# A hybrid attention and SwiGLU block on one core: three operand splits moved from VectorE to GpSimd, nine DMA copies and sums set later

## The chip, the cores and the metric

The kernel runs on 1 core of a Trainium2 chip. The metric is the device time of one execution in microseconds (us), lower is better. TensorE (PE) multiplies, VectorE (DVE), ScalarE (ACT) and GpSimd (POOL) work elementwise, and SyncE (SP) issues most DMAs. POOL also issues DMAs, those that add into DRAM among them. Every engine runs its own instructions in program order and waits on semaphores for the others.

## The reference, cut to what matters

One decoder block on 512 tokens of width 1024, float32. The part in question is the second half, after attention:

```python
h = rms_norm(x, norm2[l])
x = x + (jax.nn.silu(h @ w_gate[l]) * (h @ w_up[l])) @ w_down[l]     # D_FF = 2816
return rms_norm(x, final_norm)
```

## The kernel before

**Precision.** Each float32 operand of a matmul is split in two parts of the reduced type fp32r: a high part (a cast on ACT, `weights_hi`, L1188) and a low part, the difference of the operand and its high part. For weights the low part is taken by POOL (`split`, L765) or by DVE (`split_down` called from `split_own`, L1814). The list `by_dve` says for each chunk of weights which of the two does it. A product then takes three matmuls.

**Chunks.** The weights come in 148 chunks of 128x1024 numbers (512 KB), in one fixed order. SP loads each into one of three `raw` slots (more in the last stage). Chunk k is loaded once the low part of chunk k-3 is done, since this frees its slot. ACT casts it four chunks ahead of PE's use.

**The SwiGLU stage** has three parts. (1) Six tiles of 128 columns by plain products: chunks ("gate", f) and ("up", f), f = 0 to 5, 24 matmuls each. (2) Eight pairs of tiles in a Winograd form of Strassen's method with 7 products instead of 8: chunks ("mixed", (p, j)), p = 0 to 7 the pair and j = 0 to 6 the unit, 24 matmuls of 256 columns each. Below, m00 is ("mixed", (0, 0)), m05 is ("mixed", (0, 5)), m11 is ("mixed", (1, 1)) and so on. (3) The product with w_down, again in 7 products of 6 groups: chunks ("down", ...). The first down chunk is used after m76.

**Sums of weights.** Strassen's method needs sums of quarters of the weights. They are made in DRAM by DMA. `plan_sums` lists them as entries i = 0 to 55. An entry is a copy that SP issues (L715), right behind the load of chunk `copy_at[i]`, and then an accumulating DMA that POOL issues (`add_sum`, L786), in POOL's program behind chunk `add_at[i]`'s place. POOL waits there until the copy has landed. Entries 32 to 46 make the sums of w_down that use a copy: T3 (6 groups), T1 (6) and T2 (3). Nine more entries are added in place, later, and the change leaves them as they are.

**Order around the change.** In the loop over f on DVE, the low part of a chunk is taken four chunks ahead of PE: behind the tile f = 4 those of m00 and m01, behind f = 5 those of m02 and m03, in pair 0 at units 0, 1 and 2 those of m04, m05 and m06. `swiglu_tile(f)` (L1873 to L1883, L1820) multiplies gate and up and makes the forms for the last stage. `x_low` (L1863) takes the low parts of the activations' forms, which PE needs in pair 0: A11 and A12 behind f = 3, S2, S3 and A22 behind f = 4, S1 and S4 behind f = 5. Before `x_low` ACT makes the high parts (`x_high`, L1420), and ahead of these, at f = 4, `first_high` (L1406), which waits for L1874 on DVE. DVE's L1896 and L1905 take gate and up out of PSUM.

Of the kernel before, what the change touches and what calls it, by code (L numbers as in the profile page):

```python
# [54 lines left out]
SPLIT_SLOTS = 4  # L55
# [81 lines left out]
N_UNIT = len(UNITS)  # L137
BY_DVE = (0, 2, 4, 6)
# [39 lines left out]
def plan_chunks():  # L178

    chunks = []  # L180
    for kind, a in PROJ_JOBS:
        if kind == "h":
            chunks += [("w1", (a, q)) for q in range(4)]
        elif kind not in ("ht", "hc", "mt"):
            chunks.append((kind, a))
    chunks += [("o", (dh, kc)) for kc2 in (2, 0) for dh in range(2) for kc in (kc2, kc2 + 1)]
    fill = len(chunks)
    for f in range(F0):
        chunks += [("gate", f), ("up", f)]
    for p_ in range(N_PAIR):  # L190
        chunks += [("mixed", (p_, j)) for j in range(N_UNIT)]
    chunks += [("down", (n, g)) for n in range(N_PROD) for g in range(GROUPS_M)]
    return chunks, fill
# [29 lines left out]
def hymba_block(nc, x, norm1, w_in, lambda_q1, lambda_k1, lambda_q2, lambda_k2, diff_subln,  # L223
# [3 lines left out]
    chunks, n_fill = plan_chunks()  # L227
# [5 lines left out]
    todo = plan_sums()  # L233
    mixed0, down_from = n_fill + 2 * F0, n_fill + 2 * F0 + N_UNIT * N_PAIR
    copy_at = [6 + i for i in range(10)] + [27 + i // 2 for i in range(14)] + [KEYS_DONE] * 8
    copy_at += [n_fill + i for i in (0, 2, 4, 6, 7, 8, 9, 10, 11)] + [mixed0 + N_UNIT * i + 5 for i in range(6)]
    in_place = [down_from + GROUPS_M + i for i in range(COPIED_T2, GROUPS_M)] + [down_from + 3 * GROUPS_M + i for i in range(GROUPS_M)]
    add_at = copy_at[0:16] + [31] * 8 + [33] * 4 + [35] * 4 + copy_at[32:] + in_place
    assert len(add_at) == len(todo)
    by_dve = [c[0] == "down" or (c[0] == "mixed" and (c[1][1] in BY_DVE or c[1][0] == 0)) or (c[0] in ("gate", "up") and c[1] >= SPLIT_SLOTS // 2)  # L240
              for c in chunks]

    def late(c):
# [1789 lines left out]
```

## Time and profile before

| what | value |
|---|---|
| time, median of 3 runs | 656.55 us (656.27, 656.55, 660.47) |
| the profiled execution | 656.27 us |
| its span in the trace | 654.4 us |
| PE busy | 640.9 us |
| DVE busy | 460.0 us |
| ACT busy | 355.2 us |
| POOL busy | 246.1 us |

The profiled execution is 1.9 us longer than its span: that much lies around the first and last instruction. A busy time is the time in which at least one instruction of the engine is in flight. Matmuls overlap, so a matmul's duration is longer than the distance to the next one. Time stamps below are microseconds from the start of the span.

### The profile page before, as it was taken

The page shows a single profiled execution, that of the slowest core. Times are in us where ns is not written, and L with a number is a line of the kernel's source. Part 1 is how long each engine was busy: PE and PEld are TensorE (multiplying, and loading weights), DVE is VectorE, ACT ScalarE, POOL GpSimd, SP SyncE. Part 2 cuts the span into 40 slices and gives each one's busy share as a digit, 9 for nine tenths or more (in the row PEclk, how much of TensorE's full clock was granted, in tenths as well). Part 3 has the DMA queues.
Part 4 walks back from the last instruction along what each step waited for, and adds up shares of the span by engine and source line. Part 5 has one row for each costly group of instructions (what it writes and reads, how often), then busy time and mean ns, then how long its engine had stood idle before and what let it go on. Part 6 is the DMA issues. An engine that isn't in the chain of part 4 may idle for free.

```text
span 654.4 us, 11411 instructions
## 1 busy us (share of the span) xinstructions
PE 640.9 (98%) x4059; PEld 573.6 (88%) x4059; DVE 460.0 (70%) x956; ACT 355.2 (54%) x697; POOL 246.1 (38%) x153
## 2 busy tenths in 40 slices
PE   8999999999999999999999999999999999999996
PEld 7888988888899877888878899999999998888884
DVE  5435437746655787735479998888888898788984
ACT  7546446778664558725332474444444446655653
POOL 4766344585151533463312103434443320121522
PEclk9999999999999999999999999999999999999999
DMA  8989979569995996997399957888787678989913
GB/s 243 273 178 229 262 213 222 123 179 356 262 254 120 232 196 185 203 222 210 109 310 284 252 160 244 249 234 237 231 247 201 201 224 286 329 259 256 293 64 128
DMA packets 116007, 146.58 MB, mean 224 GB/s; under 512 B 5252, under 2 KB 73968, under 8 KB 115952
## 3 DMA queue, kind: packets, MB, share of 16 engines
q1 hardware_dynamic: 96936, 110.49, 53.7%
q0 software_dynamic: 16352, 30.84, 27.2%
q10 hardware_dynamic: 2664, 4.53, 2.0%
q8 instruction: 33, 0.54, 0.3%
q14 instruction: 22, 0.18, 0.1%
HBM read 139.53 MB, written 59.00 MB: 303 GB/s over the span
## 4 chain that ended last, share of the span: by engine, by line
PE 92%; DVE 2%; issue 2%; ACT 1%; POOL 1%; DMA 1%; POOLq 0%; ACTq 0%; DVEq 0%
PE bank L816 9%; PE bank L818 9%; PE bank L817 9%; PE bank L1147 8%; PE bank L1145 8%; PE bank L1146 8%; PE bank L835 7%; PE bank L837 7%; PE bank L836 7%; PE bank L988 6%; PE bank L964 3%; PE bank L948 2%; PE bank L949 2%; PE bank L1027 1%; DMA causal<-in_c_causal_dram 1%
## 5 line engine op out<-in xcount | busy, mean ns | idle before, releaser
L765 POOL TENSOR_TENSOR w_lo<-raw,w_hi 128x1024 fp32r<-128x1024 f32 (+1 forms) x63 | 156.2, 2483 | 227.3 <-ACT w_hi L1188 226.6
L1188 ACT CAST w_hi<-raw 128x1024 fp32r<-128x1024 f32 (+2 forms) x123 | 127.0, 1039 | 117.6 <-PE bank L1147 57.6
L1657 DVE CUSTOM_DVE_ANT_0 bank<-bank,bias 128x128 f32<-128x128 f32 (+3 forms) x96 | 47.6, 497 | 76.4 <-PE bank L949 40.5
L835 PE MATMUL bank<-xT_hi,w_hi 128*128 128x512 f32 x208 | 83.4, 401 | 0.8 <-POOL w_lo L765 0.6
L837 PE MATMUL bank<-xT_hi,w_lo 128*128 128x512 f32 x208 | 81.9, 394 | 0.0
L836 PE MATMUL bank<-xT_lo,w_hi 128*128 128x512 f32 x208 | 81.7, 393 | 0.0
L1814 DVE TENSOR_TENSOR w_lo<-raw,w_hi 128x1024 fp32r<-128x1024 f32 (+1 forms) x61 | 73.6, 1207 | 10.6 <-ACT w_hi L1188 10.4
L1145 PE MATMUL bank<-xs,w_hi 128*128 128x256 f32 x256 | 72.3, 282 | 0.0
L1147 PE MATMUL bank<-xs,w_lo 128*128 128x256 f32 x256 | 72.2, 282 | 0.0
L1146 PE MATMUL bank<-xs,w_hi 128*128 128x256 f32 x256 | 72.2, 282 | 0.0
L786 POOL DMA_DIRECT2D down_sums<-in_w_down_dram x21 | 23.3, 1109 | 109.5 <-DVE w_lo L1814 54.8
L1269 ACT ACTIVATE E<-bank,nmax 128x128 f32<-128x128 f32 (+3 forms) x80 | 42.5, 531 | 33.6 <-DVE nmax L1657 32.5
L1281 ACT COPY PT<-bank 128x384 f32<-128x384 f32 (+3 forms) x84 | 35.5, 422 | 29.6 <-PE bank L964 29.6
L1147 PEld LDWEIGHTS bank<-xs,w_lo 128*128 128x128 f32 x256 | 48.7, 190 | 0.0
L1145 PEld LDWEIGHTS bank<-xs,w_hi 128*128 128x128 f32 x256 | 48.6, 190 | 0.0
L1146 PEld LDWEIGHTS bank<-xs,w_hi 128*128 128x128 f32 x256 | 48.6, 190 | 0.0
L988 PEld LDWEIGHTS bank<-v_nsa,PT 128*128 128x128 f32 x320 | 43.4, 191 | 4.7 <-issue 1.5
L837 PEld LDWEIGHTS bank<-xT_hi,w_lo 128*128 128x128 f32 x208 | 39.1, 188 | 8.9
L835 PEld LDWEIGHTS bank<-xT_hi,w_hi 128*128 128x128 f32 x208 | 39.2, 188 | 8.8 <-issue 0.9
L836 PEld LDWEIGHTS bank<-xT_lo,w_hi 128*128 128x128 f32 x208 | 39.2, 188 | 7.3 <-issue 0.2
L988 PE MATMUL bank<-v_nsa,PT 128*128 128x64 f32 x320 | 43.4, 266 | 0.5 <-ACT bank L1293 0.3
L818 PE MATMUL bank<-w_hi,form_lo_a 128*128 128x512 f32 x98 | 38.4, 392 | 0.0
(282 smaller groups left out, 1714.5 us busy)
## 6 DMA issues: line engine op xcount, KB each, us to landing
raw<-mixed_sums SPq DMA_DIRECT2D x32, 512.0 KB, 4.4
raw<-in_w_gate_dram SPq DMA_DIRECT2D x22, 512.0 KB, 4.7
raw<-in_w_in_dram SPq DMA_DIRECT2D x20, 512.0 KB, 6.1
down_sums<-in_w_down_dram POOLq DMA_DIRECT2D x17, 512.0 KB, 8.9
mixed_sums<-in_w_up_dram SPq DMA_DIRECT2D x16, 512.0 KB, 11.2
mixed_sums<-in_w_gate_dram SPq DMA_DIRECT2D x16, 512.0 KB, 8.7
mixed_sums<-mixed_sums POOLq DMA_DIRECT2D x16, 512.0 KB, 12.9
raw<-in_w_up_dram SPq DMA_DIRECT2D x14, 512.0 KB, 4.1
```

Source lines behind the costliest of these rows:

```text
L765: nc.gpsimd.tensor_tensor(wv_lo(k)[:, 0:n], raw_at(k)[:, 0:n], wv_hi(k)[:, 0:n].bitcast(F32), ALU.subtract).then_inc(s_split, 1)
L816: nc.tensor.matmul(o, a_hi, b_hi, start=first, stop=False)
L818: return nc.tensor.matmul(o, a_lo, b_hi, start=False, stop=last)
L835: nc.tensor.matmul(bank[:, :], hi, xT_hi[:, kt, :], start=kt == 0, stop=False)
L836: nc.tensor.matmul(bank[:, :], hi, xT_lo[:, kt, :], start=False, stop=False)
L837: return nc.tensor.matmul(bank[:, :], lo, xT_hi[:, kt, :], start=False, stop=kt == KT - 1)
L988: mm = nc.tensor.matmul(bank[:, 0:v.shape[1]], PT[:, n % 2, j * P:(j + 1) * P], v, start=j == 0, stop=j == i)
L1145: nc.tensor.matmul(o, wv_hi(k)[:, w], x_hi(a)[:, kt, :], start=kt == 0, stop=False)
L1146: nc.tensor.matmul(o, wv_hi(k)[:, w], x_lo(a)[:, kt, :], start=False, stop=False)
L1147: mm = nc.tensor.matmul(o, wv_lo(k)[:, w], x_hi(a)[:, kt, :], start=False, stop=kt == 3)
L1188: nc.scalar.copy(wv_hi(k)[:, 0:n], raw_at(k)[:, 0:n]).then_inc(s_whi, 1)
L1814: nc.vector.tensor_tensor(wv_lo(k)[:, 0:n], raw_at(k)[:, 0:n], wv_hi(k)[:, 0:n].bitcast(F32), ALU.subtract).then_inc(s_dlo, 1)
```

## The change

Three things change. Of T3's entries (i = 32 to 37) the last three are set behind other chunks: all six now stand at every second gate or up chunk. The nine entries of T1 and T2 (i = 38 to 46), of which three stood at the last gate and up chunks and six at unit 5 of pairs 0 to 5, now stand at every fifth mixed chunk from m03 on (m03, m11, m16, m24, m32, m40, m45, m53, m61). And m01, m03 and m05 are no longer in `by_dve`, so their low parts are taken by POOL, as those of units 1, 3 and 5 are in the other pairs.

```diff
-    copy_at += [n_fill + i for i in (0, 2, 4, 6, 7, 8, 9, 10, 11)] + [mixed0 + N_UNIT * i + 5 for i in range(6)]
+    copy_at += [n_fill + 2 * i for i in range(6)] + [mixed0 + 3 + 5 * i for i in range(9)]
...
-    by_dve = [c[0] == "down" or (c[0] == "mixed" and (c[1][1] in BY_DVE or c[1][0] == 0)) or (c[0] in ("gate", "up") and c[1] >= SPLIT_SLOTS // 2)
+    by_dve = [c[0] == "down" or (c[0] == "mixed" and c[1][1] in BY_DVE) or (c[0] in ("gate", "up") and c[1] >= SPLIT_SLOTS // 2)
               for c in chunks]
```

DVE, from the end of tile f = 5 to unit 2 of pair 0. The first L1814 is the low part of m03, then x_low of S1 and S4, then m04, m05 and m06:

```order
 L1820 TENSOR_TENSOR form_lo_a<-form_a,high0_a 128x256
-L1814 TENSOR_TENSOR w_lo<-raw,w_hi 128x1024
 L1863 TENSOR_TENSOR xs<-form_a,xs 128x1024
 L1863 TENSOR_TENSOR x7<-form_a,x7 128x1024
 L1814 TENSOR_TENSOR w_lo<-raw,w_hi 128x1024
 L1952 TENSOR_TENSOR gate_n<-sq,bank4 128x512
-L1814 TENSOR_TENSOR w_lo<-raw,w_hi 128x1024
 L1954 TENSOR_TENSOR up_n<-sq,bank5 128x512
 L1814 TENSOR_TENSOR w_lo<-raw,w_hi 128x1024
```

The low parts of m03 and m05 have left DVE; that of m01, behind tile f = 4, has left it in the same way. What stood behind each follows at once.

POOL, from the sums behind the last gate chunk to those of pairs 2 and 3:

```order
-L786 DMA down_sums<-in_w_down_dram 128x2x512 x5
+L786 DMA down_sums<-in_w_down_dram 128x2x512 x2
+L765 TENSOR_TENSOR w_lo<-raw,w_hi 128x1024 x2
+L786 DMA down_sums<-in_w_down_dram 128x2x512
+L765 TENSOR_TENSOR w_lo<-raw,w_hi 128x1024 x2
+L786 DMA down_sums<-in_w_down_dram 128x2x512
+L765 TENSOR_TENSOR w_lo<-raw,w_hi 128x1024 x2
+L786 DMA down_sums<-in_w_down_dram 128x2x512
+L765 TENSOR_TENSOR w_lo<-raw,w_hi 128x1024 x2
 L786 DMA down_sums<-in_w_down_dram 128x512
```

After two sums POOL now takes the low parts of m01 and m03, issues the sum of entry 38 and takes those of m05 and m11; a sum stands behind every two or three low parts from there on.

## Rows read from the trace of the kernel before

**Rows 1.** The page, part 1: busy us (share of the span), instructions.
```profile
PE 640.9 (98%) x4059; PEld 573.6 (88%) x4059; DVE 460.0 (70%) x956; ACT 355.2 (54%) x697; POOL 246.1 (38%) x153
```

**Rows 2.** What PE waited for: us in total, times, longest.
```profile
PE bank L948 <- DVE E L1692: 1.6, 3, 1.0
...
PE bank L835 <- POOL w_lo L765: 0.6, 1, 0.6
```

**Rows 3.** Windows: busy of PE, PEld, DVE, ACT, POOL; PE clock, DMA share, GB/s.
```profile
350.00:360.00 10.00, 10.00 (x46) 8.16 (x45) 9.76 (x14) 1.91 (x3) 1.61 (x2) 1.00 1.12 243
...
370.00:380.00 10.00, 10.00 (x45) 8.15 (x44) 9.67 (x12) 5.30 (x7) 0.00 (x0) 1.00 0.77 202
380.00:390.00 10.00, 10.00 (x80) 9.79 (x79) 9.86 (x16) 6.43 (x8) 0.85 (x1) 1.00 0.37 117
```

**Rows 4.** PE's timeline: first matmul of m00 and of m04 (start, duration).
```profile
381.14 0.29 PE L1145 MATMUL bank<-xa,w_hi 128*128 128x256 f32 x1
...
392.62 0.28 PE L1145 MATMUL bank<-xs,w_hi 128*128 128x256 f32 x1
```

**Rows 5.** DVE's timeline, tiles f = 3 to pair 0 (start, duration, [idle before <-releaser]).
```profile
362.57 1.23 DVE L1814 TENSOR_TENSOR w_lo<-raw,w_hi 128x1024 fp32r<-128x1024 f32 x1 [1.20 <-ACT w_hi L1188]
...
375.48 0.43 DVE L1873 TENSOR_TENSOR form_a<-gate_n,up_n 128x256 f32<-128x256 f32 x1
375.82 0.42 DVE L1874 TENSOR_TENSOR up_n<-gate_n,up_n 128x256 f32<-128x256 f32 x1
376.16 1.22 DVE L1814 TENSOR_TENSOR w_lo<-raw,w_hi 128x1024 fp32r<-128x1024 f32 x1
377.67 2.36 DVE L1863 TENSOR_TENSOR xs<-form_a,xs 128x1024 fp32r<-128x1024 f32 x2 [0.29 <-ACT xs L1420]
...
383.53 0.43 DVE L1877 TENSOR_TENSOR form_a<-gate_n,up_n 128x256 f32<-128x256 f32 x1
...
386.26 1.22 DVE L1814 TENSOR_TENSOR w_lo<-raw,w_hi 128x1024 fp32r<-128x1024 f32 x1
387.40 1.22 DVE L1863 TENSOR_TENSOR xs<-form_a,xs 128x1024 fp32r<-128x1024 f32 x1
...
389.67 1.22 DVE L1814 TENSOR_TENSOR w_lo<-raw,w_hi 128x1024 fp32r<-128x1024 f32 x1
```

**Rows 6.** ACT's timeline: the casts of m01, m03, m05, and one of pair 1.
```profile
374.29 1.04 ACT L1188 CAST w_hi<-raw 128x1024 fp32r<-128x1024 f32 x1
...
382.34 1.03 ACT L1188 CAST w_hi<-raw 128x1024 fp32r<-128x1024 f32 x1
...
387.15 1.05 ACT L1188 CAST w_hi<-raw 128x1024 fp32r<-128x1024 f32 x1 [0.46 <-PE bank L1147]
...
421.48 1.05 ACT L1188 CAST w_hi<-raw 128x1024 fp32r<-128x1024 f32 x1 [0.45 <-PE bank L1147]
```

**Rows 7.** POOL's timeline in pair 1: low parts of two chunks.
```profile
416.89 2.39 POOL L765 TENSOR_TENSOR w_lo<-raw,w_hi 128x1024 fp32r<-128x1024 f32 x1 [4.83 <-ACT w_hi L1188]
422.61 2.54 POOL L765 TENSOR_TENSOR w_lo<-raw,w_hi 128x1024 fp32r<-128x1024 f32 x1 [3.32 <-ACT w_hi L1188]
```

**Rows 8.** DVE's timeline beside them.
```profile
418.59 0.69 DVE L1961 TENSOR_TENSOR up_n<-bank,up_n 128x512 f32<-128x512 f32 x1 [2.15 <-PE bank L1147]
...
422.81 2.62 DVE L1918 TENSOR_TENSOR form_a<-gate_n,up_n 128x256 f32<-128x256 f32 x1
```

**Rows 9.** DMAs into tile raw, issued from 370 to 390.
```profile
DMA to landing us min/median/max: 3.5/3.5/4.4
```

**Rows 10.** SP's copies (L715) issued from 350 to 360.
```profile
DMA to landing us min/median/max: 11.1/11.2/11.4
```

**Rows 11.** SP's copies (L715) issued from 400 to 410, one DMA.
```profile
DMA to landing us min/median/max: 6.0/6.0/6.0
```

**Rows 12.** SP's copies (L715) over the whole span.
```profile
DMA to landing us min/median/max: 3.8/8.4/21.7
```

## The prediction

> **What bounds the kernel now.** I read the busy times first: PE works for 640.9 of 654.4 us, DVE for 460.0, POOL for 246.1 [rows 1]. So PE sets the time, unless something makes it wait. Then I read what PE waited for. The longest entry is 1.6 us, on line L948, which is attention. The only wait for a low part on POOL is 0.6 us [rows 2], also ahead of the SwiGLU stage. Nothing in the list belongs to the stage that the change touches. Then the windows of that stage: PE is busy 10.00 of 10 us in each, at clock 1.00, with 45 or 46 matmuls of 512 columns in 10 us before pair 0, and never less than full [rows 3]. The same windows show DVE at 9.67 and 9.86 of 10 us, and DMA at 1.12 between 350 and 360 and only 0.37 between 380 and 390. The reader should see two things: PE can gain nothing here, since it waits for nothing and runs at its full clock; and DVE has a backlog just where pair 0 begins. So the question is whether DVE or POOL becomes late enough to stop PE.
>
> How late may they be? Pair 0 starts at 381.14 and m04, four units later, at 392.62 [rows 4], which is 2.87 us a unit. DVE finishes the low part of m04 at 389.67 + 1.22 = 390.89 [rows 5]. The margin is 392.62 - 390.89 = 1.73 us. It is the smallest that I find in this stage: m03's low part ends at 387.48 and PE needs it at 381.14 + 3 x 2.87 = 389.75, which leaves 2.27 us.
>
> **Part 1: three low parts leave DVE.** On DVE one costs 1.14 us from start to next start (386.26 to 387.40 [rows 5]). Those of m01 and m03 stand ahead of m04's, so up to 2 x 1.14 = 2.3 us leave its path. The one of m05 stands behind it and does not count.
>
> **Part 2: POOL takes them, and DVE is blocked while it does.** POOL needs 2.39 to 2.54 us for a low part. At 422.61 it starts one and ends at 425.15. DVE's L1918, which multiplies two operands in SBUF, starts at 422.81 and ends at 425.43, 0.28 us after POOL, and lasts 2.62 us [rows 7, 8]. The same operation without POOL takes 0.43 us (L1873 and L1877 [rows 5]). DVE's L1961 reads one operand from PSUM and takes 0.69 us though POOL works from 416.89 to 419.28 [rows 7, 8]. So a DVE operation with both inputs in SBUF waits for POOL's end, one with an input in PSUM does not, and a hit costs 2.62 - 0.43 = 2.2 us.
>
> The Trainium skill says this as a rule, in "SBUF — State Buffer", section "Who interferes with whom": a DVE instruction with two SBUF inputs contends with a GpSimd instruction that reads SBUF, and the lock is exclusive. By that rule each of the three moved splits hits DVE if DVE has such work then. If the two engines only shared the bandwidth, a hit would cost less and the forecast would be near the time before. The trace agrees with the rule, with the 2.62 us.
>
> Does DVE have such work at the three moments? POOL starts 0.08 us after the cast ends (421.48 + 1.05 = 422.53, start 422.61 [rows 6, 7]).
> - m01: cast ends at 375.33, POOL starts at 375.41 and ends near 377.8. DVE is to start L1873 at 375.48. Hit. L1873 and L1874 end 2.2 us later. The removed low part at 376.16 gives nothing back here, since what follows, x_low of S2 at 377.67, waits for ACT (0.29 us idle [rows 5]), and ACT waits for L1874. Sum: +2.2.
> - m03: the cast, at 382.34 before, is itself 2.2 later, ends at 385.57, and POOL works from 385.65 to 388.1. DVE is to start L1877 at 383.53 + 2.2 = 385.73. Hit: +2.2. The removed low part at 386.26 gives 1.14 back. Sum so far: 2.2 + 2.2 - 1.14 = 3.3 us.
> - m05: ACT still has to do two casts of x_high and that of m04, and one copy, then m05 (ending at 387.15 + 1.05 + 2.2 = 390.4 at the latest; its load is issued when m02's low part is done and lands in 3.5 us [rows 9]). DVE is then in the last operations of swiglu_tile or at x_low of S1. All have two inputs in SBUF, and they stand ahead of m04. Hit: +2.2. Sum: 5.5 us.
>
> So m04's low part would be ready at 390.89 + 5.5 = 396.4, against 392.62: PE would wait 3.8 us.
>
> **Part 3: the copies and sums that go from before 360 us to later.** Three copies and three sums leave the stretch of full DMA (1.12 [rows 3]), where copies took 11.1 to 11.4 us to land [rows 10]. There the load of chunk ("gate", 5) was late: ACT had to wait for it and DVE then stood idle for 1.20 us [rows 5]. I expect this idle time to go, and DVE to be 1.2 us earlier from there on; from below it may be nothing (then PE waits 3.8 us), from above it can't be more than the 1.20. I take 1.2. **The sum: 5.5 - 1.2 - 1.73 = 2.6 us of PE's waiting at m04.** PE has no slack behind it, so it stays to the end.
>
> Behind m04 I find no second wait: DVE's backlog ends there, the two units that follow have 2.9 us more margin each, and a chunk whose raw slot comes free late has 3 units, 8.6 us, for a load of 3.5 to 4.4 us [rows 9], a cast of 1.05 and a low part of 1.22 to 2.54.
>
> **Part 4: sums at other places in POOL's program.** POOL waits in a sum until its copy has landed, with the later low parts behind it. In pairs 1 to 7 the closest case is a sum one chunk ahead of POOL's next low part (m24, m32, m40). The load and copy of chunk K are issued when K-3's low part ends, and K-3 is cast when unit K-7 is done: 3 x 2.87 - 1.05 - 2.5 = 5 us before unit K-3 starts on PE. The low part of K+1 must begin by 4 x 2.87 - 2.54 = 8.9 us after that start; with 1.1 us for issuing the sum a copy may take some 12 us. In pair 1 a copy took 6.0 us [rows 11], so these cost nothing. POOL itself is idle 3.3 to 4.8 us before each low part [rows 7]; the 1.1 us of issuing fit in.
>
> The Trainium skill gives, in "SBUF — State Buffer", section "The DMA setup-cost knee", about 2 us plus the bytes at 436 GB/s for a DMA, which would make 3.2 us for 512 KB (an estimate from that page). The raw loads at 3.5 us stand near it, the crowded copies at 11.1 us don't. By its figure nothing above changes; by the crowded rows m05's cast would come after x_low of S1 and S4, and the third hit would fall away.
>
> **The forecast** is made against the profiled execution, 656.27 us (span 654.4, 1.9 around it), which is 0.3 below the median of 656.55. 656.27 + 2.6 = 658.9 us.
>
> **The rivals.**
> - *One hit less.* m05's load is late or DVE gets ahead of POOL at one of the three moments (at m01 they are 0.07 us apart, 375.41 and 375.48). Then 2.2 us less: 0.4 to 1.6 us of waiting, 656.7 to 657.9 us.
> - *DVE's relief wins.* If POOL's low parts fall beside operations that read PSUM, as at 418.59, DVE loses nothing and has 2.3 + 1.2 us more margin. PE waits for nothing before and after: 656.3 us. For it speaks that in pair 1 one of the two low parts shown missed DVE; against it, that from L1877 on DVE has ten operations in a row with SBUF inputs alone.
> - *Slower by more: POOL is held by a sum.* The sum of entry 38 stands ahead of m05's low part. Its copy is issued at about 375.4. If it took the longest landing of the trace, 21.7 us [rows 12], it would land at 397.1; with 1.1 us for issuing the sum and 2.5 for the low part m05 is ready at 400.7, while PE wants it at 392.62 + 2.87 = 395.5. PE waits 5.2 us: 661.5 us. It decides from a landing of about 16.5 us. Against it: DMA share is 0.77 and 0.37 there [rows 3], and a landing of 6 us is usual in such stretches.
> - *The change gains.* Only what PE could win in its pace; PE waits for nothing here, so below 656 only by noise.
>
> **How the numbers follow.** Three hits, 658.5 to 660.1 us: 0.50. One hit less, 656.7 to 657.9: 0.20. No waiting, 656.0 to 656.5: 0.22. POOL held, 661.5 or above: 0.05. Anything else: 0.03. The range leaves out the held POOL alone and keeps the three hits' upper case: 655.9 to 660.5 us. Within 1% of 656.55 means 650.0 to 663.1 us, and 1% is about what a measurement of this kernel can tell from no change. All cases but the extremes lie there: same 0.95, slower 0.04 (POOL held and a second wait behind it), faster 0.01.
>
> **What would show it.** In the profile after: a wait of PE at a line L1145 in pair 0, two to four us long, for DVE's L1814, at about 393. L1873 or L1874, L1877 and one of L1882, L1820 or L1863 lasting over 2 us. DVE's idle 1.20 us ahead of the split of gate 5 gone. POOL busy for three more low parts, 7.2 us. The prediction is wrong if PE does not wait in pair 0, if it waits for L765 and not L1814, or if a wait shows in later pairs.

## The result: 0.7% slower, one wait as forecast and two things behind it that were not

| what | before | after |
|---|---|---|
| time, median of 18 runs each | 657.43 us (655.27 to 661.25) | 661.60 us (658.73 to 667.38) |
| ratio after / before | | 1.0068, 95% interval 1.0044 to 1.0094 |
| the profiled execution, its span | 656.27, 654.4 us | 661.68, 659.8 us |
| its mean granted clock | 0.999 | 0.996 |

The change costs 4.2 us in the medians and 5.4 us between the two profiled executions. The forecast was 658.9 us, the upper end of its range 660.5; the median lies above that. The sign was right, the size too small: 2.6 us forecast. A part of the distance is the base: the forecast starts from 656.27 us, and the kernel before had a median of 657.43 beside this measurement, 1.2 us more. Each compared with its own base, the change cost 1.6 us more than forecast in the medians, and 2.8 between the profiled executions.

Of T3's six entries only the last two (i = 36 and 37) stand behind other chunks than before; the entry i = 35 is behind the same one. Three copies and three sums fewer are issued ahead of 360 us, as the prediction has it.

One run of low_only, below, took 698.65 us at a mean clock of 0.851, and no ratio counts it.

The busy times of the profile after, in the same columns as [rows 1]:

```profile
PE 644.7 (98%) x4059; PEld 576.4 (87%) x4059; DVE 454.8 (69%) x953; ACT 354.9 (54%) x697; POOL 253.2 (38%) x156
```

POOL has three instructions and 7.1 us more, DVE three fewer and 5.2 us less. With three low parts of 1.22 us gone and three hits of 2.2 us in their place DVE should have more, not less. The windows say where it is lower, behind pair 0. Columns as in [rows 3], before:

```profile
400.00:450.00 50.00, 50.00 (x422) 50.00 (x421) 43.01 (x51) 23.35 (x29) 22.58 (x11) 1.00 0.80 239
```

and after:

```profile
400.00:450.00 50.00, 50.00 (x422) 50.00 (x421) 37.75 (x50) 23.45 (x28) 22.66 (x12) 1.00 0.84 249
```

DVE's 43.01 us became 37.75 for one instruction less. In pairs 1 to 7 POOL takes low parts in both kernels, and DVE's operations with two SBUF inputs run into it there too ([rows 8] has one of 2.62 us). The moments shift, and each meeting costs less: counting DVE's single operations of over 1.6 us from 400 us to the end of pair 7, there are 15 in both traces, but they last 30.9 us longer than they would alone (0.43 us, or 1.22 for a low part) before and 22.7 after, 8.2 less. With the three hits and the three low parts that left, 6.6 - 3.7 - 8.2 = -5.3 us, against the -5.2 measured. copies_only, below, has 451.4 us of DVE against 460.0, with the old low parts.

PE's busy time is 3.8 us longer for the same 4059 instructions. Not all of it is slower work: before pair 0 a wait of 1.5 us for a DMA (L996, at 7 us) is there in the trace before and not in the one after. But the rest says that PE not only waited, it also worked more slowly somewhere.

What PE waited for, as in [rows 2]:

```profile
PE bank L1145 <- DVE w_lo L1814: 2.3, 1, 2.3
...
PE bank L1145 <- POOL w_lo L765: 0.8, 1, 0.8
```

Both rows are new, and both are on L1145, the first matmul of a mixed unit. The prediction named a wait in a later pair as a sign that it is wrong, and the second row is one. The windows of pair 0 after, columns as in [rows 3]:

```profile
390.00:400.00 10.00, 7.67 (x52) 7.47 (x51) 7.87 (x9) 2.04 (x3) 0.83 (x1) 0.83 0.65 179
400.00:410.00 10.00, 10.00 (x87) 10.00 (x86) 8.24 (x10) 5.90 (x7) 6.16 (x3) 1.00 0.82 226
```

In the first, PE is busy 7.67 of 10 us and does 52 matmuls, where a full window has 86 or 87. A wait of 2.33 us explains 20 of the 34 or so that are missing. The clock of 0.83 explains the others. PE's timeline shows both (start, duration, [idle before <-releaser]):

```profile
394.90 0.39 PE L1145 MATMUL bank<-xs,w_hi 128*128 128x256 f32 x1 [2.33 <-DVE w_lo L1814]
395.13 0.28 PE L1146 MATMUL bank<-xs,w_hi 128*128 128x256 f32 x1
...
396.48 0.41 PE L1145 MATMUL bank<-xs,w_hi 128*128 128x256 f32 x1
396.69 0.41 PE L1146 MATMUL bank<-xs,w_hi 128*128 128x256 f32 x1
...
399.37 0.28 PE L1145 MATMUL bank<-xs,w_hi 128*128 128x256 f32 x1
399.49 0.28 PE L1146 MATMUL bank<-xs,w_hi 128*128 128x256 f32 x1
```

Read the distance from start to start: 0.12 us at 395.13 and again from 399.0 on, 0.213 us in between. That is the lower of the clock's two levels, 1.2 instead of 2.4 GHz, from about 395.5 to 398.9. PE had stood idle for 2.33 us just before. Unit m04 takes 4.47 us instead of 2.88.

So the 5.4 us of the profiled execution come apart, from the first matmul of one unit to that of the next: m00 starts 0.2 us earlier (380.94 against 381.14 [rows 4]); from m03 to m04 5.33 us instead of 2.87, +2.5; m04 at half clock for most of its length, +1.6; two units of pair 5 around 485, +0.4; two of pair 6 around 517, +1.1. The first unit of the w_down stage starts 5.4 us later, and from there on nothing is added.

**The three hits.** DVE's timeline after, against [rows 5]:

```profile
361.11 1.22 DVE L1814 TENSOR_TENSOR w_lo<-raw,w_hi 128x1024 fp32r<-128x1024 f32 x1
...
374.01 2.60 DVE L1873 TENSOR_TENSOR form_a<-gate_n,up_n 128x256 f32<-128x256 f32 x1
...
378.37 2.36 DVE L1863 TENSOR_TENSOR xs<-form_a,xs 128x1024 fp32r<-128x1024 f32 x2 [1.43 <-ACT xs L1420]
...
384.23 2.61 DVE L1877 TENSOR_TENSOR form_a<-gate_n,up_n 128x256 f32<-128x256 f32 x1
...
388.47 2.64 DVE L1883 TENSOR_TENSOR form_a<-form_a 128x256 f32<-128x256 f32 x1
...
393.64 1.21 DVE L1814 TENSOR_TENSOR w_lo<-raw,w_hi 128x1024 fp32r<-128x1024 f32 x1
```

and POOL's, where the three new low parts stand:

```profile
373.93 2.39 POOL L765 TENSOR_TENSOR w_lo<-raw,w_hi 128x1024 fp32r<-128x1024 f32 x1 [15.12 <-ACT w_hi L1188]
384.15 2.41 POOL L765 TENSOR_TENSOR w_lo<-raw,w_hi 128x1024 fp32r<-128x1024 f32 x1 [7.83 <-ACT w_hi L1188]
386.51 1.15 POOL L786 DMA_DIRECT2D down_sums<-in_w_down_dram  x1
388.43 2.40 POOL L765 TENSOR_TENSOR w_lo<-raw,w_hi 128x1024 fp32r<-128x1024 f32 x1 [0.77 <-ACT w_hi L1188]
```

Each pair starts within 0.08 us, POOL first, and DVE's operation ends 0.3 us after POOL's: 2.60, 2.61 and 2.64 us for work of 0.43. The idle 1.20 us ahead of the split of gate 5 is gone (first row). The low part of m04 ends at 393.64 + 1.21 = 394.85, 3.96 us later than before (390.89); by the prediction's sum it was 5.5 - 1.2 = 4.3 later (0.2 of the difference is that all of DVE's work is 0.2 us earlier in this execution).

**The second wait.** The chain of work followed back from 522 us gives it in order of time (start, duration, what):

```profile
507.47 1.24 DVE w_lo L1814
...
508.72 8.66 DMA raw<-mixed_sums
...
517.41 1.05 ACT w_hi L1188
...
518.53 2.40 POOL w_lo L765
...
520.97 0.39 PE bank L1145
```

There is next to no idle time in it (the rows left out are of 0.02 to 0.07 us): a low part frees a raw slot, the load into it takes 8.66 us, the cast 1.05, the low part 2.40, and PE comes 0.83 us too early. A load was forecast at 3.5 to 4.4 us. POOL had issued a sum at 506.92 that landed in 9.7 us, beside this load. The sum alone doesn't make a load slow: before, sums were issued in this stage too, at 410.91 and every 20 us, they landed in 6.4 to 7.6 us, and no load took over 6.3. What in the new order makes both slower is open. For the raw slots between 400 and 520 us the view of one tile says what its users' engines sat idle for (us, times), before:

```profile
  PE bank L1147: 46.3, 32
  DMA raw<-mixed_sums: 16.7, 10
...
DMA to landing us min/median/max: 3.5/4.4/6.3
```

and after:

```profile
  DMA raw<-mixed_sums: 36.2, 18
  DMA raw<-in_w_gate_dram: 19.1, 11
  DMA raw<-in_w_up_dram: 12.0, 4
  PE bank L1147: 2.0, 2
...
DMA to landing us min/median/max: 3.4/5.2/8.8
```

Before, the casts mostly waited for PE to give back a high part: ACT was ahead, held by its ring. After, they wait for loads nearly always, 67.3 us against 18.3 in all. The reserve of pairs 1 to 7 is used up, though PE waits only twice.

### The profile page after: what moved, and what is told of

It is laid out like the page before. It is cut to its first block, busy times and chain, and to the rows that moved or that the text cites. A ratio compares the mean times of both kernels' runs of the same rounds, so it can differ in the third digit from the quotient of the medians.

```text
span 659.8 us, 11411 instructions
## 1 busy us (share of the span) xinstructions
PE 644.7 (98%) x4059; PEld 576.4 (87%) x4059; DVE 454.8 (69%) x953; ACT 354.9 (54%) x697; POOL 253.2 (38%) x156
## 4 chain that ended last, share of the span: by engine, by line
PE 62%; DMA 12%; DVE 12%; issue 5%; POOL 4%; ACT 4%; POOLq 0%; SPq 0%; DVEq 0%; ACTq 0%
PE bank L816 9%; PE bank L818 9%; PE bank L817 9%; DMA raw<-mixed_sums 6%; PE bank L988 5%; PE bank L835 5%; PE bank L837 5%; PE bank L836 4%; POOL w_lo L765 4%; DVE w_lo L1814 3%; PE bank L964 3%; DMA raw<-in_w_gate_dram 3%; DMA raw<-in_w_up_dram 2%; PE bank L948 2%; ACT w_hi L1188 2%
## 5 line engine op out<-in xcount | busy, mean ns | idle before, releaser
L765 POOL TENSOR_TENSOR w_lo<-raw,w_hi 128x1024 fp32r<-128x1024 f32 (+1 forms) x66 | 163.3, 2478 | 243.6 <-ACT w_hi L1188 242.7
L1814 DVE TENSOR_TENSOR w_lo<-raw,w_hi 128x1024 fp32r<-128x1024 f32 (+1 forms) x58 | 74.1, 1278 | 34.5 <-ACT w_hi L1188 34.5
L1145 PE MATMUL bank<-xs,w_hi 128*128 128x256 f32 x256 | 73.1, 286 | 3.2 <-DVE w_lo L1814 2.3
L1146 PE MATMUL bank<-xs,w_hi 128*128 128x256 f32 x256 | 72.9, 285 | 0.0
L1145 PEld LDWEIGHTS bank<-xs,w_hi 128*128 128x128 f32 x256 | 49.4, 193 | 3.6 <-DVE w_lo L1814 2.5
L1146 PEld LDWEIGHTS bank<-xs,w_hi 128*128 128x128 f32 x256 | 49.3, 193 | 0.0
```

Of the source, the lines that this page charges most:

```text
L765: nc.gpsimd.tensor_tensor(wv_lo(k)[:, 0:n], raw_at(k)[:, 0:n], wv_hi(k)[:, 0:n].bitcast(F32), ALU.subtract).then_inc(s_split, 1)
L1145: nc.tensor.matmul(o, wv_hi(k)[:, w], x_hi(a)[:, kt, :], start=kt == 0, stop=False)
L1146: nc.tensor.matmul(o, wv_hi(k)[:, w], x_lo(a)[:, kt, :], start=False, stop=False)
L1814: nc.vector.tensor_tensor(wv_lo(k)[:, 0:n], raw_at(k)[:, 0:n], wv_hi(k)[:, 0:n].bitcast(F32), ALU.subtract).then_inc(s_dlo, 1)
```

## The experiments

Each kernel was timed in rounds beside the one before on the same chip; ratios are to the kernel before. Line numbers in rows are those of each kernel. Three theories of what lies behind the first wait. First: nothing, PE's wait of 2.6 us is all. Second: the clock falls behind the wait. Third: the new places of copies and sums make loads late, and PE waits again later. The expectations name theories by letters; each says in its own text what its letters stand for.

**1 and 2. One half of the change at a time.** low_only has the new `by_dve` and the old `copy_at`; copies_only the other way round.

> The kernel before with only the low parts of m01, m03 and m05 moved to GpSimd; the copies stay where they were. Theory A (the moved low parts block VectorE three times, and PE's wait at m04 brings a stretch at half clock): three VectorE operations over 2 us in pair 0, m04's low part at about 396, PE waits 3.7 us there (2.5 in the changed kernel plus the 1.2 us of VectorE's idle time, which stays here), m04 takes about 4.5 us instead of 2.9: 5.3 us in all, ratio 1.007 to 1.009. Theory B (the new places of copies and sums delay the weights): PE waits under 1 us and the ratio is under 1.002.

> The kernel before with only the copies and sums at their new places; m01, m03 and m05 stay on VectorE. Theory A: VectorE's idle 1.20 us is gone, m04's low part is ready at about 389.7, PE waits for nothing in pair 0; ratio 0.998 to 1.001. Theory B: the waits of a few tenths to 1 us in pairs 5 and 6 that the changed kernel shows come from the copies, so they stay here, 1 to 2 us in all, ratio 1.002 to 1.003, and casts wait for loads as often as in the changed kernel.

low_only: 1.0083 [1.0059, 1.0108], as much as the whole change, with all three hits (2.60, 2.62, 2.63 us on L1873, L1877, L1883). copies_only: 1.0001 [0.9987, 1.0015], no wait in pair 0. So the low parts cost the time and the new places alone cost nothing. Theory B's 1.002 to 1.003 was missed, though what it says of the loads is there: casts wait for loads for 68.2 us between 400 and 520 us, none of them for PE, loads take up to 9.1 us, and PE waits 0.3 us in all. Late loads alone use up the reserve and don't yet stop PE. Of low_only, what PE waited for and the window behind m04:

```profile
PE bank L1145 <- DVE w_lo L1814: 2.3, 1, 2.3
```
```profile
390.00:400.00 10.00, 7.68 (x65) 7.48 (x63) 8.09 (x9) 2.63 (x3) 1.84 (x2) 1.00 0.60 147
```

The wait is 2.3 us and not the expected 3.7, since DVE's idle time ahead of the split of gate 5 is absent in this execution. It is the exception: of the six traces with the old places, this one has none and the five others 1.20, 1.49, 1.65, 1.80 and 1.85 us. The same wait leaves the clock at 1.00 here, with 65 matmuls in the window instead of 52: this execution took 658.87 us. It is the fastest of low_only's runs; the others, at mean clocks of 0.993 and 0.994, took 660.05 to 664.96. With the idle time of the other five traces their first wait would be 3.5 to 4.2 us (an estimate, 2.3 + 1.2 to 1.85); no trace of them shows it.

**3. m05_back: the third hit taken out.** After, with m05 back on DVE.

```diff
-    by_dve = [... (c[0] == "mixed" and c[1][1] in BY_DVE) ...
+    by_dve = [... (c[0] == "mixed" and (c[1][1] in BY_DVE or c[1] == (0, 5))) ...
```

> The changed kernel with m05's low part on VectorE again: two low parts on GpSimd in pair 0, not three. Theory A: two operations over 2 us, m04's low part 2.2 us earlier at about 392.6, PE waits 0 to 0.4 us in pair 0, no half-clock stretch: 4 us of the 5.4 are gone, ratio 1.000 to 1.003. Theory B, or a theory in which each moved low part costs by itself: two thirds of the cost stay, ratio about 1.005.

1.0044 [1.0028, 1.006], median 659.72, above the 1.000 to 1.003 of theory A. Two hits; the wait at m04 shrinks to 0.3 us (3.14 from m03 to m04), as 2.2 us less should make it. But PE waits elsewhere:

```profile
PE bank L1145 <- POOL w_lo L765: 2.1, 2, 1.7
```

The longer one is at m15: a sum's DMA was issued at 403.07, its load at 404.7, and the load took 9.2 us.

**4. m05_back_old: the same with the old copies.**

> The kernel before with the low parts of m01 and m03 on GpSimd, m05's on VectorE, and the copies at their old places. With the copies at their new places this had ratio 1.0044, with a wait of 1.9 us in pair 1 behind a load that took 9 us. If that wait comes from the new places of copies and sums, it is gone here: PE waits 0.3 to 1.5 us at m04 and nowhere else, ratio 1.000 to 1.002. If it comes from the moved low parts, the ratio is again 1.004.

1.003 [1.0014, 1.0047], median 658.17. No later wait, loads at most 6.3 us. The ratio is above the 1.000 to 1.002 expected. The wait at m04 is 1.8 us, against 0.3 to 1.5 expected and 0.3 in m05_back, since DVE stood idle here:

```profile
363.14 1.23 DVE L1814 TENSOR_TENSOR w_lo<-raw,w_hi 128x1024 fp32r<-128x1024 f32 x1 [1.65 <-ACT w_hi L1188]
```

Between 3 and 4 both sides of the new places show. They take away the idle time, 1.5 us of the wait at m04, and they bring the late loads: waits behind m04 with the new places, none with the old ones.

**5. fill: PE kept at work during the wait.** After, with 20 matmuls into m04's bank, which the unit then overwrites, ahead of the wait for its low part.

```diff
+                    fill = p_ == 0 and j == 4
...
+                    if fill:
+                        high_done(pe, k)
+                        for _ in range(20):
+                            nc.tensor.matmul(bank[:, 0:HALF], wv_hi(k)[:, 0:P], x_hi(a)[:, 0, :], start=True, stop=True)
+                        low_done(pe, k)
```

> The changed kernel with 20 matmuls of 256 columns added on PE just ahead of m04, into the bank that m04 then overwrites; 20 x 0.12 = 2.4 us, as long as PE's wait there. They do no work. Theory A with the clock: PE stays busy, its granted clock stays 1.00, and m04 takes 2.9 us instead of 4.5, so the time is 1.6 us shorter than the changed kernel's, ratio 1.003 to 1.005. If the slow m04 has another cause (operands late, a full queue), it still takes 4.5 us and the ratio is that of the changed kernel, 1.007.

```profile
390.00:400.00 10.00, 10.00 (x85) 9.86 (x83) 8.20 (x9) 2.59 (x3) 1.16 (x1) 1.00 0.68 166
```

m04 now takes 2.98 us, and the mean clock is 0.998 or 0.999 in all six runs, against 0.990 to 0.999, mostly 0.992 to 0.996, in 25 runs of the kernel after. The means settle the clock; the 2.98 us alone would not, since m04 took as long in low_only with no fill. The time is another matter: 1.0063 [1.004, 1.0086], runs of 658.42 to 663.55, where 1.003 to 1.005 was expected. With the clock held there is still something that varies by 5 us. copies_only varies as much, 655.12 to 659.84 at clocks of 0.997 to 0.999, while the runs of the kernel before at 0.997 or above, beside all the experiments, lie between 655.0 and 658.3. That points to the new places and their late loads; no experiment separates it.

**6. after_again: a control.** The kernel after once more, on the chip of the next five.

> The changed kernel once more, as the measure for the three beside it on the same chip: ratio about 1.007, PE's wait of 2.4 to 2.5 us at m04 in any profile of it, mean granted clock 0.990 to 0.999.

1.0063 [1.0041, 1.0085], clocks 0.993 to 0.995. Its profiled execution is the other way round from the first: no fall behind m04, but a second wait of 1.9 us at the second unit of pair 5, with the fall behind that one:

```profile
PE bank L1145 <- DVE w_lo L1814: 2.3, 1, 2.3
PE bank L1145 <- POOL w_lo L765: 1.9, 1, 1.9
```
```profile
480.00:490.00 10.00, 8.15 (x67) 7.94 (x66) 6.27 (x9) 3.80 (x5) 3.04 (x2) 0.97 0.77 221
490.00:500.00 10.00, 10.00 (x75) 10.00 (x75) 9.42 (x12) 2.89 (x4) 5.57 (x3) 0.86 0.96 254
```

**7 and 8. small_sums and small_sums_fill: the spread DMAs made small.** The copies and sums of the nine spread entries move an eighth of their bytes. What is left out: seven eighths of these sums and of three that build on them, and the products of w_down that would use a sum read a quarter of w_down itself, as many bytes. small_sums_fill has the 20 matmuls of fill as well.

```diff
-                    sp.dma_start(sum_part(i, ("sum", to)), sum_part(i, ("w",) + begin))...
+                    cut = slice(0, 64 if i >= 38 else None)
+                    sp.dma_start(sum_part(i, ("sum", to))[:, :, cut], sum_part(i, ("w",) + begin)[:, :, cut])...
...
-                pool.dma_start(sum_part(i, ("sum", to)), sum_part(i, add), accum_op=ALU.add,
+                cut = slice(0, 64 if 38 <= i < 47 or 50 <= i < 53 else None)
+                pool.dma_start(sum_part(i, ("sum", to))[:, :, cut], sum_part(i, add)[:, :, cut], accum_op=ALU.add,
```

> The changed kernel with the DMAs of the nine spread copies and sums (and of three later sums that read them) cut to 64 of 512 columns, an eighth of their bytes; every instruction, wait and place stays. The down chunks that would read the sums read w_down itself, so the last product is another one. Theory C (a load of weights that runs beside a sum's or a copy's DMA lands in 7 to 9 us, and this makes the later waits of PE): loads land in 3.5 to 5 us, no wait of PE behind m04, the casts wait for PE again and not for loads; the wait of 2.4 us at m04 and the clock behind it stay: ratio 1.005 to 1.006. Theory D (the lateness behind m04 feeds itself, because SP loads in order): casts go on waiting for loads, and PE's later waits stay: ratio 1.007.

> The same cut in bytes and, in addition, the 20 idle matmuls ahead of m04. If the cost is the sum of three things, 2.5 us of waiting at m04, the stretch at half clock behind it and waits from late loads, only the first is left: 2.5 us, ratio 1.0035 to 1.0045, and all runs within 1 us of each other with a granted clock of 0.998 or more. If it stays above 1.006, there is a cost that I don't know.

small_sums: 1.0049 [1.0029, 1.0069], median 659.35: theory C's ratio within its interval, and its loads. The raw slots' view, 400 to 520 us:

```profile
  PE bank L1150: 60.8, 40
  DMA raw<-in_w_gate_dram: 3.2, 2
  DMA raw<-mixed_sums: 1.6, 1
...
DMA to landing us min/median/max: 3.4/4.0/5.0
```

Loads land in 5.0 us at most, the casts wait for loads 4.8 us instead of 67.3, and PE waits nowhere behind m04. There it waits 2.3 us and the clock falls (0.83 in 390 to 400). small_sums_fill: 1.0047 [1.0025, 1.0069], where 1.0035 to 1.0045 was expected; median 659.07, which is 2.6 above the median before. Loads land in 5.6 us at most. Its profiled execution has a span of 656.8, exactly 2.4 above 654.4, and the only thing left in it is the 5.30 us from m03 to m04. Ten of its twelve runs lie between 657.82 and 660.02; the two others (660.75 and 665.86, clock 0.992) I can't explain; all within 1 us was expected. So in the traces the second and the third theory both hold: what is left of this profiled execution is the wait of 2.4 us, all that the first has. That the fill is what kept the clock in it rests on the mean clocks, 0.997 or more in 10 of 12 runs against 3 of 8 without the fill. In the times the four ratios of 5 to 8 are not told apart: their intervals overlap.

**9 and 10. pool_reads and pool_writes: the hit by itself.** The kernel before, with work on POOL at the places of the three low parts that nobody waits for: one subtraction of 128x1024 with both inputs in SBUF, or two memsets of the same tile (the last line of the diff).

```diff
+                if chunks[k] in [("mixed", (0, j)) for j in (1, 3, 5)]:
+                    high_done(pool, k)
+                    nc.gpsimd.tensor_tensor(high0_a[:, 3:7, :]..., xT_hi[:, 0:2, :]..., xT_lo[:, 0:2, :]..., ALU.subtract)
...
+                        nc.gpsimd.memset(high0_a[:, 3:7, :].bitcast(F32), 0.0)
```

> The kernel before, every low part of pair 0 on VectorE and the copies at their old places. GpSimd does three subtractions of 128x1024 in addition, with both inputs in SBUF, released like the low parts of m01, m03 and m05 by their casts; nobody waits for the results. If it is the reading of SBUF by GpSimd that holds VectorE, three VectorE operations last over 2 us and m04's low part is later by 3 x 2.2 us with nothing taken off VectorE: 390.9 + 6.6 = 397.5, so PE waits about 4.9 us at m04 (3.7 if VectorE has no idle 1.20 us): ratio 1.006 to 1.010. If what costs is only that the low parts come late from GpSimd, nothing changes here: ratio 1.000.

> The same as the run with the subtractions, with two memsets of 128x1024 in the place of each: GpSimd is busy and writes SBUF at the same moments, but reads nothing. By the rule that only GpSimd's reads hold a VectorE operation with two SBUF inputs, no VectorE operation is longer than 1.3 us in pair 0 and the ratio is 1.000. If any work of GpSimd on SBUF holds VectorE, PE waits at m04 as with the subtractions.

pool_reads: 1.0114 [1.0097, 1.013], above the 1.006 to 1.010 expected. Three operations are hit. DVE's rows, PE's wait, and the window:

```profile
376.67 2.60 DVE L1882 TENSOR_TENSOR form_a<-gate_n,up_n 128x256 f32<-128x256 f32 x1
...
386.90 2.62 DVE L1886 TENSOR_TENSOR form_a<-gate_n,up_n 128x256 f32<-128x256 f32 x1
...
391.14 2.57 DVE L1892 TENSOR_TENSOR form_a<-form_a 128x256 f32<-128x256 f32 x1
```
```profile
395.24 0.58 PE L1154 MATMUL bank<-xs,w_hi 128*128 128x256 f32 x1 [4.79 <-DVE w_lo L1823]
```
```profile
390.00:400.00 10.00, 5.21 (x28) 5.01 (x28) 9.93 (x11) 1.01 (x2) 3.13 (x2) 0.66 0.38 84
```

PE waits 4.8 us, but at m03 and not at m04, so that it is near the 4.9 expected is luck. m03's low part is on DVE here, behind the same three hits, and ends at 395.2 (before: 387.5), where PE wanted it first. Behind the wait m03 runs at half clock for most of its length and takes 4.77 us, 1.9 more than before. The unit ahead, with the wait, is 5.0 us longer than before; together 6.9 of the 7.4 us between the spans.

pool_writes: 1.0000 [0.9984, 1.0015]. POOL is busy for 1.97 us at each of the three places, no single operation of DVE between 375 and 392 us lasts over 1.22 us, and beside the first memsets DVE has:

```profile
375.33 1.97 POOL L800 MEMSET high_a<- 128x1024 f32 x2 [8.28 <-ACT w_hi L1197]
```
```profile
375.43 0.43 DVE L1882 TENSOR_TENSOR form_a<-gate_n,up_n 128x256 f32<-128x256 f32 x1
```

The same DVE operation, starting within 0.1 us after POOL in both: 2.60 us beside a read, 0.43 beside a write. This shows what Part 2 only argued. It's no lack of POOL's or DVE's time, it is POOL's reads of SBUF. The Trainium skill says in "SBUF — State Buffer", section "Who interferes with whom", that such a DVE instruction does not contend with a GpSimd instruction that only writes; pool_writes agrees with it.

**11 and 12. Is there a better version?** In each mixed unit the eight matmuls of the first half that use only the high part come ahead of the wait for the low part. This gives every low part about 1 us more.

```diff
-                    low_done(pe, k)
+                    high_done(pe, k)
...
+                        if z == 0:
+                            low_done(pe, k)
```

> The kernel before with another order of each mixed unit's matmuls on PE: the 8 that need no low part of the weights first in the first half of the unit, and only then the wait for the low part. The low parts may then be 8 x 0.12 = 0.95 us later. The profile of before shows no wait to hide, so 1.000; if short waits behind late loads make up the spread of its runs (655.0 to 660.2), they shrink and the ratio is 0.997 to 0.999.

> The changed kernel with the same other order of matmuls. PE's wait at m04 shrinks by 0.95 us from 2.4 to 1.5, the later waits of 0.3 to 2 us by up to 0.95 each: ratio 1.003 to 1.004 in the place of 1.0065, and if a shorter wait also spares the half clock, the granted clock is 0.997 or more in most runs.

On the kernel before 1.0009 [0.9996, 1.0021]: nothing to gain, PE waits for nothing there. On the kernel after 1.007 [1.0037, 1.0103], median 659.82, runs of 657.83 to 665.73; its profiled execution is its longest run. The wait at m04 shrank to 1.4 us as expected, with no fall of the clock behind it; three later ones of 0.6, 1.2 and 0.9 us follow. And pair 0 begins at 385.45, 4.5 us later than in after: the clock fell to 0.89 between 0 and 10 us and to 0.84 between 250 and 260, in stages that neither the change nor this order touches. So a low mean clock need not come from the waits. The time isn't told apart from after's, and 1.003 to 1.004 was missed. No version beats the kernel before.

## Why the prediction was wrong in size

**Part 1, the relief of DVE:** right. The split of m01 gave nothing back: DVE stood idle 1.43 us ahead of x_low for ACT, where it had been 0.29 [rows 5].

**Part 2, three hits of 2.2 us:** right in number and size, and in place: L1873, L1877, and for the third L1883, which stands between the L1882 and L1820 that were named. pool_reads and pool_writes show the cause. The split of m04 was 3.96 us later, 4.3 by the sum.

**Part 3, minus 1.2 us:** right, and the reason too. In the six traces with the old places the loads of gate 5 and up 5, issued around 351 to 354 us, took 8.8 to 12.5 us to land, and in five of the six DVE stood idle, for 1.20 to 1.85 us. In the eight with the new places the same two loads took 4.3 to 6.8 us, and DVE stood idle there in none. The pair m05_back and m05_back_old shows it at PE: a wait of 0.3 us against 1.8. The 1.0001 of copies_only doesn't speak against it, since with all low parts on DVE there is no wait at m04 that could shrink. The 1.20 of the sum is the smallest of the five.

**The first wait:** 2.6 forecast, 2.46 measured.

**"PE has no slack behind it, so it stays to the end":** this step failed in size. The wait stayed, and it grew. Behind it PE ran at the lower clock for 3.4 us, 1.6 us lost. The term that stands for the wait should have been the wait and what the clock takes behind it, 0 to 1.6 us for each wait of about 2 us in these traces. Over 25 runs of after the mean clock is 0.9944 on average, over the 25 runs of before on the same chip as after_again 0.9973: 0.0029 x 655 = 1.9 us a run (an estimate), behind this wait, a later one, or elsewhere. 2.4 + 1.9 us is near the 4.2 measured, but fill (above) doesn't bear that sum out.

**"Behind m04 I find no second wait":** this step failed. A second wait of 0.8 us stands in pair 6 of after, one of 1.9 in pair 5 of after_again. The step took 3.5 to 4.4 us for a load [rows 9], from a stretch with hardly any sums. The kernel after spreads copies and sums over pairs 0 to 7, where loads take up to 8.8 us. The working was: 8.6 us for a load, a cast and a low part. 8.66 + 1.05 + 2.40 = 12.1 us is above that. What kept PE from more waits is that casts run ahead, which [rows 6] shows in ACT's idle of 0.45 for PE; that reserve went from 46.3 us of waiting for PE to 2.0. Something else shows in SP: it loads in program order. m04's low part frees the slot for m10, m05's that for m11, and m04's now came after m05's. Timeline of SP after:

```profile
386.58 0.37 SPq L701 DMA_DIRECT2D raw<-in_w_up_dram  x1
394.88 0.92 SPq L701 DMA_DIRECT2D raw<-in_w_gate_dram  x2
```

m11's slot had been free since POOL finished m05 at 390.83, but its load stood behind m10's, and both left together at 394.88. So no load was issued for 8.3 us. By itself this brings no second wait: low_only and small_sums have the same gap of 8.3 us, loads of 6.4 and 5.0 us at most from 400 to 520 us, and no wait of PE behind m04. Nor do late loads alone: copies_only has loads of up to 9.1 us and 0.3 us of waiting. The longer later waits are all in traces that have late loads and moved low parts (after, after_again, fill, m05_back). That the gap is what the moved low parts add is argued, not shown.

**What stays open.** low_only (1.0083) is not below the whole change (1.0068 and 1.0063), though it has no late loads. DVE's idle time, which stays with the old places, would account for 1.2 to 1.85 us of it; but the intervals overlap, and low_only's one trace is the one without it. How much of the 4.2 us is the clock and how much are later waits, in the mean, is not settled: fill and small_sums_fill hold the clock at 0.997 to 0.999 in 16 of 18 runs, and their intervals still overlap with that of after. What is shown: the first wait of 2.4 us is there in the traces of after, low_only, after_again and small_sums; each of the two additions appears in traces and goes with its own cure; and small_sums_fill, with both cures, is 2.4 us above before in its trace and 2.6 in its median (3.1 by its ratio, with an interval of 1.6 to 4.5).

**The rivals.** One hit less is what m05_back and m05_back_old are: 659.72 us with the new places and 658.17 with the old ones, both above the 656.7 to 657.9 given for it. DVE's relief didn't win. POOL held by a sum did not occur at m05: its low part started at 388.43, 0.08 us after its cast.

## What to carry to other kernels

Moving elementwise work to an idle GpSimd is not free when it reads SBUF and the busy VectorE has operations with two SBUF inputs there: each meeting costs VectorE the rest of GpSimd's operation, here 2.2 us for an operation of 0.43 that starts just behind it. When a forecast finds a wait of TensorE of about 2 us, add what the granted clock may take behind it, here 0 to 1.6 us, and widen the range upwards. State the forecast as a difference and compare it with the kernel before as timed beside the new one. And when DMAs are spread over a stage with a short ring of buffers, take a load's duration from beside such DMAs, not from a quiet stretch, and see whether in-order loads bunch behind the late one.

## What was not expected of the hardware

- The same wait of 2.3 us is followed by half clock for 3.4 us in one execution (after, small_sums) and by none in another (low_only, after_again). The wait of 4.8 us in pool_reads is followed by half clock, those of 1.8 in m05_back_old and 1.4 in after_hi_first are not. The mean clock changes from run to run of one kernel: after ranges from 658.73 us at 0.999 to 667.38 at 0.990. With twenty matmuls in the wait it was 0.998 or 0.999 in all six runs of fill.
- A 512 KB load takes 3.4 us at best. With copies and accumulating DMAs from DRAM to DRAM at the new places the slowest between 400 and 520 us took 8.5 to 9.3 us, at the old places 6.3 to 7.1, but 8.5 in pool_reads, and with both kinds of DMA cut to an eighth 5.0 and 5.6.
- GpSimd's memsets, 1.97 us beside a VectorE operation with two SBUF inputs, cost it nothing; GpSimd's subtraction in the same place costs 2.2 us.
